# Pool stage by token tiles: own banks for each tile's causal sums, and the band matrix loaded through ScalarE's queue

## The chip, the cores and the metric

The kernel runs on one core of a Trainium2 chip. The time is the device time of one execution in microseconds, median of three runs. The engines are TensorE (PE, with its weight loads as PEld), VectorE (DVE), ScalarE (ACT), GpSimd (POOL) and SyncE (SP), which here only issues transfers. Each runs its own instructions in order and waits on semaphores for the others.

## What is computed

Two stacks of two layers each, on 256 tokens of width 1024, in float32. The first layer's mixer is the part that the change touches: a normalised input, a causal window mean minus the input itself per group of 256 channels (windows 2, 4, 8, 16), one 256x256 product per group, a scale, and the residual.

```python
def pool_mixer(h, w, scale):                 # h = rmsnorm(x, norm_mixer[0])
    csum = concat([zeros, cumsum(h, axis=1)])
    for g, win in enumerate((2, 4, 8, 16)):
        start = maximum(t + 1 - win, 0)
        window_sum = csum[:, 1:, sl] - take(csum[:, :, sl], start)
        outs.append(window_sum / cnt - h[:, :, sl])
    d = stack(outs, axis=2)
    return einsum('btgc,gce->btge', d, w).reshape(B, T, D) * scale

x = x + pool_mixer(...)
x = x + swiglu(rmsnorm(x, norm_ffn[0]), w_gate_up[0], w_down[0])
```

Behind it come a block attention layer and the second stack (three kinds of attention with a latent one, two layers), each with a SwiGLU network. All that is unchanged.

## The kernel before

Tokens lie in two tiles (t = 0, 1) of 128. Every product is made of three float32r matmuls of high and low parts (`three`, lines 1617 to 1619): hi x hi, hi x lo, lo x hi. So an operand has a high half, written by ScalarE (`h_hi`, `whi`), and a low half, the rounding error, written by VectorE (`h_lo`, `wlo`). PSUM has 8 banks of 512 float32 columns; four of them, `ACC` = 4 to 7, hold the stage's output, one for each token tile and half of the width.

The head of the kernel, up to about 23 us, is the pool stage:

- SyncE issues x (two tiles), the gain rows, the band matrix, the pool weights in two halves, the pool scale, then weight units of the first network and many small constants (L516 onwards). GpSimd issues the identity (L612) and two tables.
- The band holds the window weights of each group, 160 columns: 128 for a tile's own tokens, 16 for those of the next tile that still look back into it, and more. VectorE multiplies it by the tokens' 1/rms (`scaled_band`, L1350, L1355), so one matmul with x as weights gives normalised causal sums with channels on partitions (L1817). Tile 0's matmuls are 144 columns wide, to reach the first 16 tokens of tile 1; those of tile 1 are added on top. Banks 0 to 3 hold one group each, both tiles side by side, and a group is ready (`pool_d`) only when tile 1's matmuls are through.
- ScalarE evicts a group with the gain as scale (L832), both tiles at once, and VectorE makes its low half (L1385). ScalarE splits the pool weights' high part in two halves (L824, `pool_whi`), VectorE the low part (L1376, `pool_wlo`).
- PE multiplies (L1617 to L1619), tile and group in the order (0,0), (1,0), (0,1), (1,1), (0,2), (0,3), (1,2), (1,3): 48 matmuls of 256 columns.
- VectorE scales each output (L1139, `pool_scale`) and adds it to x (L1147, `pool_add`); ScalarE squares, VectorE and GpSimd make 1/rms, VectorE normalises (L1046), PE transposes (L1787), and ScalarE and VectorE evict again (L706, L1053) for the first network's weights (L1721).
- To fill time and keep PE at work there are matmuls with zeros (`multiply_zeros`, L1804): 10 and 5 ahead of the causal sums, 6 and 5 behind the pool matmuls, with a small table matmul (L1841) between the last two.

The order on each engine is the order in the text. VectorE's order behind the sums is written in `first_norm`.

Of the kernel before, what the change touches and what calls it, by code (L numbers as in the profile page):

```python
# [24 lines left out]
F32 = mybir.dt.float32  # L25
# [165 lines left out]
def bass_two_stacks(nc, a, c, out):  # L191
    ctx = ExitStack()
    with ctx:
# [3 lines left out]
        def sem(name):  # L197
            return ctx.enter_context(nc.semaphore(name))
# [81 lines left out]
        banks = ctx.enter_context(nc.psum_tensor("bank", [P, 8, HALF], F32))  # L280
        bank = [banks[:, i, :] for i in range(8)]
        ACC = [4, 5, 6, 7]


        vec_dram = nc.dram_tensor("vec_scratch", [24, SEQ_D], F32, kind="Internal")
# [4 lines left out]
        hi_ready, lo_ready, units_used = sem("hi_ready"), sem("lo_ready"), sem("units_used")  # L290
        x_in = [sem("x_in0"), sem("x_in1")]
        small_in, scale_in, ident_in = sem("small_in"), sem("scale_in"), sem("ident_in")
        pool_w_in, pool_hi, pool_lo, pool_out = sem("pool_w_in"), sem("pool_hi"), sem("pool_lo"), sem("pool_out")
        gain_turned, gcol_ready, last_square = sem("gain_turned"), sem("gcol_ready"), sem("last_square")
        table_in, onehot_in = sem("table_in"), sem("onehot_in")
# [159 lines left out]
        def _(sp):  # L455
# [59 lines left out]
            for t in range(TT):  # L515
                sp.dma_start(x[:, t, :], xv[t]).then_inc(x_in[t], 16)  # L516
            sp.dma_start(gain_rows, GAIN_SRC[0].rearrange("(k p) -> k p", p=P)).then_inc(gains_in[0], 16)
            sp.dma_start(band, c["c_band"].rearrange("p g n -> p (g n)")).then_inc(band_in, 16)
            pool_w = raw[:, 0, :].rearrange("p (g k n) -> p (g k) n", g=4, k=2)
            for part, landed in enumerate((pool_w_in, raw_in[0])):  # L520
                sp.dma_start(pool_w[:, 4 * part:4 * part + 4, :],
# [158 lines left out]
        def _(act):  # L680
            def split(n, b=0):

                s = slot_of(n)
                act.wait_ge(raw_in[s], 16 * (n // SLOTS + 1 + b))
                if not (isinstance(b, int) and n + 3 * b < SLOTS):
                    act.wait_ge(units_used, n - 2 + 3 * b)
                w = width_of(n) if isinstance(n, int) else UNIT
                act.activation(whi[:, s, 0:w], raw[:, s, 0:w], ACT.Copy).then_inc(hi_ready, 1)  # L688
# [20 lines left out]
            def norm(j, square_too=True, late_split=None, by_tile=False):  # L709

                by_tile = by_tile or late_split is not None
                for t in range(TT):
                    for h in range(2):
                        if square_too:
                            square(NORM_X[j], t, h)
                    if t == 0 and by_tile:
                        if late_split is not None:
                            split(late_split)
                        for h in range(2):
                            h_out(j, 0, h)  # L720
                for t in range(1 if by_tile else 0, TT):
                    for h in range(2):
                        h_out(j, t, h)
# [88 lines left out]
            act.wait_ge(zeros_set, 1)  # L812
            act.activation(junk[:, 0:T], o_lo[:, 0, :].bitcast(F32), ACT.Square).then_inc(warmed, 1)
            act.wait_ge(warmed, 1)
            for t in range(TT):
                square(0, t, 0, 2)
            act.wait_ge(gain_turned, 1)
# [2 lines left out]
            def pool_whi(part):  # L820

                act.wait_ge((pool_w_in, raw_in[0])[part], 16)
                cols = slice(part * UNIT // 2, (part + 1) * UNIT // 2)
                act.activation(whi[:, 0, cols], raw[:, 0, cols], ACT.Copy).then_inc((pool_hi, hi_ready)[part], 1)  # L824

            act.wait_ge(gcol_ready, 1)
            for k in range(4):
                if k % 2 == 0:
                    pool_whi(k // 2)
                act.wait_ge(pool_d, k + 1)  # L830
                for c_ in (2 * k, 2 * k + 1):
                    i = act.activation(h_hi[:, c_, :], bank[k][:, (c_ % 2) * T:(c_ % 2 + 1) * T], ACT.Copy, scale=gcol[:, c_:c_ + 1])  # L832
                i.then_inc(hT_hi, 1)
            split(1)
            ffn(0)


# [164 lines left out]
        def _(dve):  # L1002
# [108 lines left out]
            def lambdas():  # L1111
# [11 lines left out]
                    dve.tensor_scalar(subln_s[:, l:l + 1], subln[:, l:l + 1], 1.0 - init, None, ALU.mult).then_inc(lam_done, 1)  # L1123
                dve.wait_ge(lam_done, 2)

            def ffn(f):
                u0, e0, g0 = FFN_U[f], NB * f, (NB - 1) * f
                j = [1, 4, 7, 9][f]

                def pool_scale(t, h):  # L1130

                    no = 2 * t + h
                    if no == 0:
                        dve.wait_ge(scale_in, 16)
                    if no < 3:
                        dve.wait_ge(acc_ready, (1, 3, 2)[no])
                    else:
                        dve.wait_ge(units_used, POOL_U + 1)
                    dve.tensor_tensor(pool_y[:, no, :], bank[ACC[no]][:, :],  # L1139
                                      pt[:, h, :], ALU.mult).then_inc(pool_out, 1)  # L1140

                def pool_add(t, h):
# [6 lines left out]
                def first_norm():  # L1149

                    pool_scale(0, 0)
                    pool_add(0, 0)
                    pool_scale(0, 1)
                    pool_add(0, 1)
                    pool_scale(1, 0)
                    mean_square(1, 0)
                    pool_add(1, 0)
                    normalise(1, 0, 0)
                    normalise(1, 0, 1)
                    pool_scale(1, 1)  # L1160
                    pool_add(1, 1)
                    h_lo_out(1, 0, 0)
                    h_lo_out(1, 0, 1)
                    mean_square(1, 1)
                    split_part(u0, 0, 4)
                    normalise(1, 1, 0)
                    normalise(1, 1, 1)
                    for part in range(1, 4):
                        split_part(u0, part, 4)
                    h_lo_out(1, 1, 0)  # L1170
                    h_lo_out(1, 1, 1)
                    split(u0 + 1)
# [190 lines left out]
            second_half_square(0)  # L1363
            dve.wait_ge(last_square, 1)
            mean_square(0, 0)
            second_half_square(1)
            scaled_band(0)
            dve.wait_ge(last_square, 2)
            mean_square(0, 1)
            scaled_band(1)  # L1370

            def pool_wlo(part):
# [3 lines left out]
                dve.tensor_tensor(wlo[:, 0, cols], raw[:, 0, cols], whi[:, 0, cols].bitcast(F32),  # L1376
                                  ALU.subtract).then_inc((pool_lo, lo_ready)[part], 1)

            dve.wait_ge(gcol_ready, 1)
            for k in range(4):  # L1380
                if k % 2 == 0:
                    pool_wlo(k // 2)
                dve.wait_ge(hT_hi, k + 1)
                for c_ in (2 * k, 2 * k + 1):
                    i = dve.scalar_tensor_tensor(out=h_lo[:, c_, :], in0=bank[k][:, (c_ % 2) * T:(c_ % 2 + 1) * T],  # L1385
                                                 scalar=gcol[:, c_:c_ + 1], in1=h_hi[:, c_, :].bitcast(F32),
                                                 op0=ALU.mult, op1=ALU.subtract)
                i.then_inc(hT_lo, 1)
            ffn(0)

            for ev in moba_script():
# [222 lines left out]
        def _(pe):  # L1614
# [187 lines left out]
            def multiply_zeros(n, bk):  # L1802
                for _i in range(n):
                    pe.matmul(bank[bk][:, :], o_lo[:, 0, 0:P], o_lo[:, 0:2, :], start=True, stop=True)  # L1804
# [4 lines left out]
            pe.wait_ge(gains_in[0], 16)  # L1809
            pe.transpose(bank[7][:, 0:KC], gain_rows, ident[0:KC, 0:KC]).then_inc(gain_turned, 1)  # L1810
            multiply_zeros(IDLE_MATMULS[1], 6)
            for s in range(TT):
                width, stride, at = (P, P, P) if s else (P + 16, BAND_W, 0)
                pe.wait_ge(xn_ready, 2 * s + 2)
                for g in range(4):
                    for k in range(2):
                        mm = pe.matmul(bank[g][:, k * T + at:k * T + at + width], x[:, s, g * 256 + k * P:g * 256 + (k + 1) * P],  # L1817
                                       band_s[s][:, g * stride:g * stride + width],
                                       start=(s == 0 and k == 0), stop=(s == 1 and k == 1), skip_group_check=True)
                    if s:  # L1820
                        mm.then_inc(pool_d, 1)
            hi, lo = w8(POOL_U)
            for t, g in ((0, 0), (1, 0), (0, 1), (1, 1), (0, 2), (0, 3), (1, 2), (1, 3)):
                if t == 0:
                    if g % 2 == 0:
                        pe.wait_ge((pool_lo, lo_ready)[g // 2], 1)
                    pe.wait_ge(hT_lo, g + 1)
                for k in range(2):
                    mm = three(bank[ACC[2 * t + g // 2]][:, (g % 2) * 256:(g % 2) * 256 + 256],
                               h_hi[:, 2 * g + k, tile(t)], h_lo[:, 2 * g + k, tile(t)],  # L1830
                               hi[:, 2 * g + k, :], lo[:, 2 * g + k, :], k == 0, k == 1)
                if g % 2 and (t, g) != (1, 3):
                    mm.then_inc(acc_ready, 1)
            used(mm)

            multiply_zeros(IDLE_MATMULS[2], 3)
            pe.wait_ge(ones_set, 2)
            pe.wait_ge(table_in, 32)
            pe.wait_ge(onehot_in, 16)
            pe.wait_ge(pool_out, 3)  # L1840
            pe.matmul(bank[6][0:24, :], tables[:, :], onehots, start=True, stop=True).then_inc(vec_done, 1)  # L1841
            multiply_zeros(IDLE_MATMULS[3], 3)

            def ffn(f):
                u0, e0 = FFN_U[f], NB * f
# [378 lines left out]
```

## Time and profile before

| | us |
|---|---|
| median of 3 runs (1120.51 to 1120.81) | 1120.54 |
| the profiled execution in all | 1121.29 |
| its span, first to last instruction | 1118.9 |
| PE busy | 1107.7 (99%) |
| VectorE busy | 789.5 (71%) |
| ScalarE busy | 539.2 (48%) |

The page divides the span into 40 slices and gives the busy share of each engine in tenths, with the clock that TensorE was granted. The chain of work that ended last is followed back from the last instruction to what released each step. "Busy" of PE is modelled: matmuls overlap, so that 128x256 ones that last 0.28 us each start 0.12 us apart.

### The profile page before, as it was taken

The page shows a single profiled execution, that of the slowest core. Times are in us where ns is not written, and L with a number is a line of the kernel's source. Part 1 is how long each engine was busy: PE and PEld are TensorE (multiplying, and loading weights), DVE is VectorE, ACT ScalarE, POOL GpSimd, SP SyncE. Part 2 cuts the span into 40 slices and gives each one's busy share as a digit, 9 for nine tenths or more (in the row PEclk, how much of TensorE's full clock was granted, in tenths as well). Part 3 has the DMA queues.
Part 4 walks back from the last instruction along what each step waited for, and adds up shares of the span by engine and source line. Part 5 has one row for each costly group of instructions (what it writes and reads, how often), then busy time and mean ns, then how long its engine had stood idle before and what let it go on. Part 6 is the DMA issues. An engine that isn't in the chain of part 4 may idle for free.

```text
span 1118.9 us, 16758 instructions
## 1 busy us (share of the span) xinstructions
PE 1107.7 (99%) x6429; PEld 963.2 (86%) x6429; DVE 789.5 (71%) x1032; ACT 539.2 (48%) x709; POOL 97.1 (9%) x184
## 2 busy tenths in 40 slices
PE   8999999999999999999999999999999999999997
PEld 7888888898888888888998888888899988888886
DVE  6866666767667666678886676666778867766675
ACT  5533333455654333336785543333456755333332
POOL 2000000000000000001660000000036400000000
PEclk9999999999999999999999999999999999999999
DMA  8865565673358556655963465557489444655551
GB/s 258 266 207 191 177 211 189 216 239 113 116 173 278 190 184 200 210 176 145 268 200 118 165 226 188 187 187 217 144 203 264 134 146 161 213 190 187 187 187 37
DMA packets 175974, 211.21 MB, mean 189 GB/s; under 512 B 24467, under 2 KB 159187, under 8 KB 175922
## 3 DMA queue, kind: packets, MB, share of 16 engines
q1 hardware_dynamic: 166146, 202.89, 56.8%
q0 software_dynamic: 9776, 7.62, 3.7%
q8 instruction: 34, 0.56, 0.2%
q14 instruction: 18, 0.15, 0.0%
HBM read 201.98 MB, written 1.16 MB: 182 GB/s over the span
## 4 chain that ended last, share of the span: by engine, by line
PE 96%; DVE 1%; issue 1%; ACT 0%; DMA 0%; POOL 0%; SPq 0%; DVEq 0%; POOLq 0%; ACTq 0%
PE bank L1643 26%; PE bank L1647 14%; PE bank L1617 13%; PE bank L1618 13%; PE bank L1619 13%; PE bank L1721 4%; PE bank L1929 2%; PE bank L1950 2%; PE bank L1656 1%; PE bank L1787 1%; PE bank L1960 1%; PE bank L1682 1%; PE bank L1713 1%; PE bank L1659 1%; PE bank L1964 1%
## 5 line engine op out<-in xcount | busy, mean ns | idle before, releaser
L688 ACT ACTIVATE whi<-raw 128x2048 fp32r<-128x2048 f32 (+2 forms) x180 | 342.0, 1903 | 387.3 <-PE bank L1647 244.9
L1016 DVE TENSOR_TENSOR wlo<-raw,whi 128x2048 fp32r<-128x2048 f32 x175 | 398.2, 2278 | 145.1 <-ACT whi L688 144.7
L1643 PE MATMUL bank<-h_both,whi 128*128 128x512 f32 x1280 | 304.6, 390 | 0.0
L1643 PEld LDWEIGHTS bank<-h_both,whi 128*128 128x128 f32 x1280 | 237.7, 188 | 47.8
L1617 PE MATMUL bank<-whi,o_hi 128*128 128x512 f32 (+1 forms) x452 | 177.4, 392 | 0.0
L1618 PE MATMUL bank<-wlo,o_hi 128*128 128x512 f32 (+1 forms) x452 | 176.0, 389 | 0.0
L1619 PE MATMUL bank<-whi,o_lo 128*128 128x512 f32 x448 | 174.4, 389 | 0.0
L1647 PEld LDWEIGHTS bank<-h_both,wlo 128*128 128x128 f32 x1280 | 164.1, 191 | 6.2
L1647 PE MATMUL bank<-h_both,wlo 128*128 128x256 f32 x1280 | 166.0, 283 | 0.0
L1617 PEld LDWEIGHTS bank<-whi,o_hi 128*128 128x128 f32 x452 | 85.1, 188 | 17.6 <-issue 1.3
L1619 PEld LDWEIGHTS bank<-whi,o_lo 128*128 128x128 f32 x448 | 84.1, 188 | 17.9
L1618 PEld LDWEIGHTS bank<-wlo,o_hi 128*128 128x128 f32 x452 | 85.1, 188 | 15.5
L1221 DVE TENSOR_REDUCE pr<-bank 128x512 f32<-128x1024 f32 x40 | 48.9, 1223 | 47.5 <-PE bank L1647 47.5
L1226 DVE TENSOR_REDUCE pr<-bank 128x512 f32<-128x1024 f32 x36 | 44.1, 1224 | 42.9 <-PE bank L1647 42.9
L622 POOL TENSOR_TENSOR rstd<-msq,neghalf 128x1 f32<-128x1 f32 x16 | 9.6, 599 | 742.1 <-DVE msq L1034 742.1
L1617 PE MATMUL bank<-h_both,whi 128*128 128x256 f32 x192 | 54.8, 286 | 0.0
L796 ACT ACTIVATE pr<-pr,negmax 128x256 f32<-128x256 f32 (+1 forms) x96 | 45.9, 480 | 18.0 <-DVE negmax L1311 18.0
L1618 PE MATMUL bank<-h_both,whi 128*128 128x256 f32 x192 | 54.3, 283 | 0.0
L1619 PE MATMUL bank<-h_both,wlo 128*128 128x256 f32 x192 | 54.3, 283 | 0.0
L1311 DVE CUSTOM_DVE_ANT_0 pr<-bank,bias 128x256 f32<-128x256 f32 (+1 forms) x96 | 32.8, 397 | 12.2 <-PE bank L1929 9.6
L1721 PE MATMUL bank<-whi,h_both 128*128 128x512 f32 x160 | 39.6, 395 | 0.4 <-ACT h_both L706 0.3
L1617 PE MATMUL bank<-whi,h_both 128*128 128x256 f32 (+1 forms) x128 | 39.0, 304 | 0.6 <-DVE h_both L1385 0.6
(202 smaller groups left out, 1330.3 us busy)
## 6 DMA issues: line engine op xcount, KB each, us to landing
raw<-in_w_gate_up SPq DMA_DIRECT2D x44, 1024.0 KB, 5.1
raw<-in_w_down SPq DMA_DIRECT2D x44, 1024.0 KB, 4.9
raw<-in_w_gate SPq DMA_DIRECT2D x22, 1024.0 KB, 5.4
raw<-in_w_up SPq DMA_DIRECT2D x22, 1024.0 KB, 5.3
raw<-in_w_in SPq DMA_DIRECT2D x18, 1024.0 KB, 6.7
raw<-in_w_o SPq DMA_DIRECT2D x12, 1024.0 KB, 4.9
raw<-in_w_kv SPq DMA_DIRECT2D x8, 1024.0 KB, 5.4
raw<-in_w_q SPq DMA_DIRECT2D x4, 1024.0 KB, 5.2
```

Source lines behind the costliest of these rows:

```text
L688: act.activation(whi[:, s, 0:w], raw[:, s, 0:w], ACT.Copy).then_inc(hi_ready, 1)
L796: e = act.activation(pr[:, s, q, 0:w], src, ACT.Exp, bias=negmax[:, s, q:q + 1], scale=-1.0 if biased else 1.0, accum_out=psumrow[:, s, q: ...
L1016: dve.tensor_tensor(wlo[:, s, 0:w], raw[:, s, 0:w], whi[:, s, 0:w].bitcast(F32), ALU.subtract).then_inc(lo_ready, 1)
L1221: dve.tensor_reduce(gate32, halves(0), AX_X, ALU.add).then_inc(gate_sum, 1)
L1226: dve.tensor_reduce(up32, halves(2), AX_X, ALU.add).then_inc(up_sum, 1)
L1311: e = dve.tensor_tensor_reduce(pr[:, s, q, 0:w], bank[i % 2][:, q * T:q * T + w], biases[q], -1.0, BIG, ALU.add, ALU.min, negmax[:, s, q:q ...
L1617: pe.matmul(dst, ahi, bhi, start=first, stop=False)
L1618: pe.matmul(dst, ahi, blo, start=False, stop=False)
L1619: return pe.matmul(dst, alo, bhi, start=False, stop=last)
L1643: pe.matmul(bank[bk + jj][:, :], hi[:, kc, jj * P:(jj + 1) * P], h_both[:, kc, :, :].rearrange("p a t -> p (a t)"), start=(kc == 0), stop= ...
L1647: mm = pe.matmul(bank[bk + jj][:, T:2 * T], lo[:, kc, jj * P:(jj + 1) * P], h_hi[:, kc, :], start=False, stop=(kc == KC - 1))
L1721: mm = pe.matmul(bank[bk][:, :], h[:, kc, tile(t)], pair_of(w, n, kc), start=(first and kc == 0), stop=(last and kc == KC - 1))
```

## The change

Banks: tile 0's own sums go to banks 0 to 3 (256 columns each), tile 1's to banks 6 and 7 (two groups each). The outputs go to `POOL_ACC` = 4, 5, 2, 3. Tile 0's matmuls lose their 16 extra columns, which become eight matmuls of their own into banks 6 and 7. Tile 0 is evicted, given its low half and multiplied as its groups come; tile 1's eviction follows on ScalarE behind both weight halves, and its low half on VectorE behind the scale and add of both halves of tile 0. PE multiplies all of tile 0, then all of tile 1. The split of the first network's first unit moves on ScalarE behind the squares of tile 0. The band's transfer is issued by ScalarE instead of SyncE. VectorE scales the band for tile 0 ahead of the second tile's squares. The idle matmuls behind the stage write bank 0 in place of bank 3, and a wait on `pool_out` ahead of the table matmul goes.

```diff
+        POOL_ACC = [4, 5, 2, 3]
@@ SyncE
-            sp.dma_start(band, c["c_band"]...).then_inc(band_in, 16)
@@ ScalarE: norm(j=1), after the squares of tile 0
                     if t == 0 and by_tile:
+                        if j == 1:
+                            split(FFN_U[0])
                         if late_split is not None:
                             split(late_split)
@@ ScalarE
             act.wait_ge(warmed, 1)
+            act.dma_start(band, c["c_band"]...).then_inc(band_in, 16)
+            def pool_t0_h_hi(g):
+                act.wait_ge(pool_d, g + 1)
+                for k in range(2):
+                    i = act.activation(h_hi[:, 2 * g + k, 0:P], bank[g][:, k * P:(k + 1) * P], ACT.Copy, scale=gcol[...])
+                i.then_inc(pool_t0_hi, 1)
+            def pool_t1_h_hi(half):
+                act.wait_ge(pool_d, 4 + half + 1)
+                for k in range(4):
+                    c_ = 4 * half + k
+                    i = act.activation(h_hi[:, c_, P:2 * P], bank[6 + half][:, k * P:(k + 1) * P], ACT.Copy, scale=gcol[...])
+                i.then_inc(hT_hi, 2)
             act.wait_ge(gcol_ready, 1)
-            for k in range(4):
-                if k % 2 == 0:
-                    pool_whi(k // 2)
-                act.wait_ge(pool_d, k + 1)
-                for c_ in (2 * k, 2 * k + 1):
-                    i = act.activation(h_hi[:, c_, :], bank[k][:, (c_ % 2) * T:(c_ % 2 + 1) * T], ACT.Copy, scale=gcol[...])
-                i.then_inc(hT_hi, 1)
-            split(1)
+            pool_t0_h_hi(0)
+            pool_t0_h_hi(1)
+            pool_whi(0)
+            pool_t0_h_hi(2)
+            pool_t0_h_hi(3)
+            pool_whi(1)
+            pool_t1_h_hi(0)
+            pool_t1_h_hi(1)
@@ VectorE: pool_scale
-                        dve.wait_ge(acc_ready, (1, 3, 2)[no])
+                        dve.wait_ge(acc_ready, (1, 2, 3)[no])
-                    dve.tensor_tensor(pool_y[:, no, :], bank[ACC[no]][:, :],
+                    dve.tensor_tensor(pool_y[:, no, :], bank[POOL_ACC[no]][:, :],
@@ VectorE: first_norm
                     pool_scale(0, 0)
                     pool_add(0, 0)
                     pool_scale(0, 1)
                     pool_add(0, 1)
+                    pool_t1_h_lo(0)
+                    mean_square(1, 0)
+                    pool_t1_h_lo(1)
+                    normalise(1, 0, 0)
                     pool_scale(1, 0)
-                    mean_square(1, 0)
+                    normalise(1, 0, 1)
                     pool_add(1, 0)
-                    normalise(1, 0, 0)
-                    normalise(1, 0, 1)
                     pool_scale(1, 1)
                     pool_add(1, 1)
@@ VectorE: head (pool_t0_h_lo(g): two 128x128 residuals of group g; pool_t1_h_lo(half): four)
             mean_square(0, 0)
+            scaled_band(0)
             second_half_square(1)
-            scaled_band(0)
             dve.wait_ge(last_square, 2)
             mean_square(0, 1)
+            pool_t0_h_lo(0)
             scaled_band(1)
-            (for each k: pool_wlo(k // 2) if k is even; two 128x256 residuals)
+            pool_t0_h_lo(1)
+            pool_wlo(0)
+            pool_t0_h_lo(2)
+            pool_t0_h_lo(3)
+            pool_wlo(1)
@@ PE
-            (tile 0: 8 matmuls of 144 columns; tile 1: 8 of 128; banks 0 to 3)
+            pe.wait_ge(xn_ready, 2)
+            for g in range(4):
+                for k in range(2):
+                    mm = window(g, k * P, 0, 2 * g + k, g * BAND_W, P, k == 0, k == 1)
+                mm.then_inc(pool_d, 1)
+            pe.wait_ge(gcol_ready, 1)
+            for half in range(2):
+                for k in range(4):
+                    window(6 + half, k * P, 0, 4 * half + k, (2 * half + k // 2) * BAND_W + P, 16, k == 0, False)
+            pe.wait_ge(xn_ready, 4)
+            for half in range(2):
+                for k in range(4):
+                    mm = window(6 + half, k * P, 1, 4 * half + k, (2 * half + k // 2) * P, P, False, k == 3)
+                mm.then_inc(pool_d, 1)
-            for t, g in ((0, 0), (1, 0), (0, 1), (1, 1), (0, 2), (0, 3), (1, 2), (1, 3)):
+            for t, g in ((0, 0), (0, 1), (0, 2), (0, 3), (1, 0), (1, 1), (1, 2), (1, 3)):
-                    pe.wait_ge(hT_lo, g + 1)
+                pe.wait_ge((pool_t0_lo, hT_lo)[t], g + 1)
-            multiply_zeros(IDLE_MATMULS[2], 3)
+            multiply_zeros(IDLE_MATMULS[2], 0)
-            pe.wait_ge(pool_out, 3)
             pe.matmul(bank[6][0:24, :], tables[:, :], onehots, start=True, stop=True).then_inc(vec_done, 1)
-            multiply_zeros(IDLE_MATMULS[3], 3)
+            multiply_zeros(IDLE_MATMULS[3], 0)
```

## Rows read from the trace of the kernel before

**Rows 1.** The page: busy time of PE, and the granted clock in 40 slices.
```profile
PE 1107.7 (99%) x6429; PEld 963.2 (86%) x6429; DVE 789.5 (71%) x1032; ACT 539.2 (48%) x709; POOL 97.1 (9%) x184
...
PEclk9999999999999999999999999999999999999999
```

**Rows 2.** Waits of PE, whole kernel: total us, times, longest.
```profile
PE bank L1804 <- DVE o_lo L1339: 1.5, 1, 1.5
...
PE bank L1617 <- DVE h_both L1385: 0.6, 1, 0.6
PE bank L1682 <- DVE h_both L1053: 0.6, 1, 0.6
```

**Rows 3.** Chain that ended last, in order of time: start us, us, what.
```profile
8.92 2.69 PE bank L1817 x20
...
11.62 0.85 ACT h_both L832 x2
...
12.49 0.89 DVE h_both L1385 x2
...
13.52 0.36 PE bank L1617
...
19.51 1.39 PE bank L1804 x6
...
23.22 0.45 PE bank L1787 x4
```

**Rows 4.** Timeline, 0 to 20 us: start us, us, engine, line, operation [idle before].
```profile
0.75 0.86 SPq L516 DMA_DIRECT2D x<-in_x  x2
...
1.47 4.53 PE L1804 MATMUL bank<-o_lo 128*128 128x512 f32 x10 [1.47 <-DVE o_lo L1339]
...
2.04 0.42 ACT L813 ACTIVATE junk<-o_lo 128x256 bf16<-128x256 f32 x1
2.08 0.36 SPq L518 DMA_DIRECT2D qall<-in_c_band  x1
...
4.08 0.69 DVE L1360 CUSTOM_DVE_ANT_0 xn<-x 128x512 f32<-128x512 f32 x1 [2.39 <-DMA x<-in_x]
...
6.63 0.22 PE L1810 MATMUL bank<-ident,xn 8*128 8x8 f32 x1 [0.62 <-DMA ident<-in_c_ident]
6.78 1.43 PE L1804 MATMUL bank<-o_lo 128*128 128x512 f32 x5
...
8.31 0.55 DVE L1350 TENSOR_SCALAR qall<-qall,rstd 128x640 f32<-128x640 f32 x1 [1.79 <-issue]
...
8.92 4.01 PE L1817 MATMUL bank<-qall,x 128*128 128x144 f32 x32 [0.70 <-DVE qall L1350]
...
9.58 1.06 ACT L824 ACTIVATE whi<-raw 128x1024 fp32r<-128x1024 f32 x1 [2.52 <-DMA raw<-in_pool_w]
...
10.74 1.23 DVE L1376 TENSOR_TENSOR wlo<-raw,whi 128x1024 fp32r<-128x1024 f32 x1 [0.47 <-ACT whi L824]
11.62 1.56 ACT L832 ACTIVATE h_both<-bank,gcol 128x256 fp32r<-128x256 f32 x4 [0.99 <-PE bank L1817]
12.49 1.66 DVE L1385 SCALAR_TENSOR_TENSOR h_both<-bank,gcol,h_both 128x256 fp32r<-128x256 f32 x4 [0.53 <-ACT h_both L832]
...
16.88 0.68 DVE L1139 TENSOR_TENSOR pr<-bank,pt 128x512 f32<-128x512 f32 x1
...
18.20 0.68 DVE L1139 TENSOR_TENSOR pr<-bank,pt 128x512 f32<-128x512 f32 x1
```

**Rows 5.** DMA issues, 0 to 40 us: KB each, median us to landing.
```profile
ident<-in_c_ident POOLq DMA_DIRECT2D x1, 64.0 KB, 5.3
```

**Rows 6.** Weight loads by form, whole kernel: busy us, mean ns.
```profile
L1817 PEld LDWEIGHTS bank<-qall,x 128*128 128x128 f32 x32 | 3.8, 191 | 1.1 <-DVE qall L1350 1.1
...
L1962 PEld LDWEIGHTS bank<-pt,vg 128*64 128x64 f32 x32 | 2.8, 137 | 0.8
...
L1841 PEld LDWEIGHTS bank<-bias,tables 97*24 97x24 f32 x2 | 0.1, 101 | 0.4 <-issue 0.4
```

## What the change was expected to do, before it ran

> **What bounds the kernel now.** The page comes first: PE is busy for 99% of the span, and its granted clock stands in the top tenth in all forty slices [rows 1]. So time can be won or lost only where PE waits, or where its queue grows or shrinks. The waits of PE come next [rows 2], each named by the instruction that waited and what it waited for: 1.5 us at the start, 0.6 before the first pool matmul (L1617), and over the rest of the kernel nothing longer than 0.6 us; the timeline adds 0.6 before the identity is there and 0.7 before the first causal sum [rows 4]. Nothing behind the pool stage has slack that could swallow a shift: what the stage loses or wins arrives at the end one for one. The chain of waits is then read for the first 30 us [rows 3]. It runs through the band's transfer (it ends DVE's wait at 8.31), the causal-sum matmuls (8.92), ScalarE's eviction (11.62), VectorE's residual (12.49), 48 pool matmuls from 13.52 to 19.51 (0.36 for the first, so 0.12 for each of 47), and then 11 idle matmuls round the table matmul, up to 23.22, where the transposes of the next norm start. What is on this chain is the whole argument.
>
> **Band and start of the sums.** Let T be the start of the first causal-sum matmul, now 8.92. Three things bound it: the band has landed (8.31, then 0.61 for the scaling and the hand-over), tile 0 is normalised (earlier), and PE is through its own queue. PE waits for the identity until 6.63, then runs five idle matmuls, 6.78 to 8.21 [rows 4]. By their pitch of 0.23 us it could take the next work near 8.05. ScalarE now issues the band after its warm-up at 2.04 + 0.42, about 0.4 us later than SyncE did at 2.08, but it no longer stands behind x in one queue. Bounds for its landing: above, as now, 8.31; below, 2.5 plus the 3.3 us that x's first tile took from issue (0.75) to use (4.08), 5.8 [rows 4]. I take 7.2, the middle. Then the band no longer decides and PE's own queue does: T = 8.05, or a little later if the identity, which shares the transfers' engines with a further queue, is late. I take T = 8.2, with 8.05 and 8.92 as ends. The issue itself, near 0.4 us on ScalarE, is hidden: that engine next waits for x's first tile, which VectorE too has only at 4.08 [rows 4]. SyncE's queue moves up by the same 0.4 us; the pool weights still come after the same bytes, so I leave them at 9.58.
> The Trainium skill (DMA: Bandwidth & Descriptors, Queues, rings and completion order) says that each DMA engine goes round the queues that have work, so a new queue gets a share at once. By that rule 7.2 is right and x's second tile is delayed instead; no row here has such a transfer of this size.
>
> **Causal sums.** Removed: 8 matmuls of 144 columns; added: 8 of 128 and 8 of 16. Each shows as two records, so 32 become 48. Twenty records take 2.69 us and all 32 take 4.01, so the last twelve, 128 wide, cost 0.11 each; the 144-wide cost 0.124 [rows 3, 4]. The trace has no 16-column matmul. Its columns alone would be priced by the difference, 0.014 us a record. But every one needs a weight load of 128 columns, and loads of 24, 64 and 128 columns last 101, 137 and 191 ns [rows 6]: 0.86 ns a column, so 0.11 us of loading each, which is also the pitch of the 128-wide ones. I take 0.11 and keep 0.014 as the lower end (16 records: 1.76 or 0.2 us). From T to the first pool matmul, S: 48 x 0.11 + 0.15 = 5.45, so S = 13.65.
> Beside it: the first group's sums are ready at T + 0.72 (2.69 less 0.44 and 15 x 0.124 leaves 0.39 for the first record, three more). of 128x256 evictions on ScalarE two take 0.85 us and four 1.56, of residuals on VectorE 0.89 and 1.66 [rows 3, 4]: pitches of 0.36 and 0.39, and 0.50 for one alone. No 128x128 one exists; less the 0.11 and 0.13 of 128 columns they would be 0.26, at worst 0.36 and 0.39, at best 0.20. VectorE's order is residual, the band's second half, residual, wlo (1.23), two residuals, wlo: the first wlo is done at T + 4.2, the second at T + 6.5 (its whi, 1.06 us a half [rows 4], is done at T + 5). The first wlo is hidden behind the sums, which are 1.2 us longer. The second is wanted by the 13th pool matmul at S + 1.44 = T + 6.9, so it is hidden too, by 0.3 us; if that goes, PE waits.
>
> **The second tile's wait.** This is the step that decides. Now the pool matmuls alternate between tiles; h_lo of all four groups is made before any VectorE work on the outputs, and PE never stops. After the change PE does all of tile 0 (24 matmuls), then waits for tile 1's residual, which stands on VectorE behind two scale and two add instructions of tile 0. The second scale waits for the 24th matmul itself. So:
> first pool matmul S; 24th done S + 0.36 + 23 x 0.12 = S + 3.1; scale and add, 18.20 - 16.88 = 1.32 from one scale to the next [rows 4], S + 4.45; four 128x128 residuals, 3 x 0.26 + 0.34, S + 5.55; hand-over 0.14, as now from 12.49 + 0.89 to 13.52 [rows 3], S + 5.7; 24 matmuls, 0.35 + 23 x 0.12, S + 8.8.
> Now the last is done at 19.51, which is S' + 6.0 with S' = 13.52. So PE stops for 2.8 us that no filler covers, with S + 2.9 to S + 5.7 idle. The second half's residual (a mean square of 0.2 and four residuals) is done 1.25 us after the first, inside the 1.44 us of PE's twelve matmuls.
>
> **Behind it.** The fillers and the table matmul come after the pool matmuls in PE's order, and their count stands: 23.22 - 19.51 = 3.71 us, unchanged. The dropped wait on pool_out never showed. Tile 0's normalised rows are ready near S + 9, well under the fillers, so what the change frees in that place buys nothing: the fillers were long enough. Scale and add of tile 1 hide there as well (3 us of cover). Behind 23.22 the order is as now, with the next norm's first weights split late enough on ScalarE to be hidden by 4 us.
> Sum: 2.8 + (13.65 - 13.52) = +2.95 us. The profiled execution has a span of 1118.9 and took 1121.29 in all, 0.75 above the median of 1120.54; its analogue after would have a span near 1121.9. On the median: 1120.54 + 2.95 = 1123.5.
>
> **Rivals.**
> A. The forecast, T 8.05 to 8.5 and prices as taken: +2.7 to +3.3, 1123.2 to 1123.8.
> B. Not slower: narrow instructions cost only their columns. Place: the 16 small records on PE, and the 128x128 residuals on VectorE. Price: with 0.014 instead of 0.11, S is set by the first wlo and the 13th matmul by the second, as if S were T + 5.1 (-0.35); residuals at 0.20 take 0.25 off the second tile's wait and 0.5 off the way to the second wlo. With T = 8.05: 2.8 + (13.15 - 13.52) - 0.75 = +1.7, 1122.2. It decides once it gives back 0.75 us. For it: the columns are half and an eighth. Against it: rows 6 for the loads.
> C. The band or the identity is no earlier, or later: T = 8.92 to 9.5. Then +3.7 to +4.25, 1124.2 to 1124.8. For it: transfers issued by GpSimd beside x took 5.3 us for 64 KB [rows 5], so a queue of its own is no guarantee of speed.
> D. The clock. The first ten idle matmuls, after an idle start, took 4.53 us against 1.43 for five later ones [rows 4], 0.45 each against 0.23 to 0.29: at half speed at first, though the page's clock row stays high. If the 2.8 us stop brings that back, 24 matmuls of 256 columns at 0.21 instead of 0.12 cost 2.2 us more, +5.1, 1125.7. The Trainium skill (TensorE: Matmul & The Clock Gate, HAM oscillation) warns of just this, waits between bursts that put the clock back; of the trace of before only the start bears on it, and PE was busy before this stop, where it was cold there.
> E. Something unseen, such as the 0.6 us waits downstream falling away: 0 to -3 us.
>
> **Chances.** A 0.56, B 0.16, C 0.14, D 0.10, E 0.04. A measurement of this kernel tells some 0.2% (2.24 us) from no change. Faster has half of E, 0.02. Within 0.2% is up to 1122.8: B nearly whole and the other half of E, 0.18. Slower: 0.80. The range takes in A, B and C and ends below D: 1122.0 to 1125.1.
>
> **What would show it.** In the new trace: the band scaled before 8.0 and the sums from about 8.2; 48 sum records over 5.4 us; a stop of PE near 16.6 to 19.4, ended by VectorE's residual; the last pool matmul near 22.4 and the transposes near 26.1. I am wrong if the stop is under 1.5 us, if the small matmuls run at a pitch far from 0.11, or if the transposes start within 1 us of 23.2.

## The result

The changed kernel takes 1128.77 us (median of 6 runs, 1127.62 to 1132.32) against 1120.55: ratio 1.008, interval 1.0069 to 1.009, so 8.2 us slower, where 3.0 were forecast, the range ended at 1125.1 and the dearest rival was priced at 5.1. The profiled execution took 1128.51 with a span of 1126.3; before, 1121.29 and 1118.9.

Waits of PE over the whole kernel, after (answers to [rows 2]):

```profile
PE bank L1655 <- DVE h_both L1160: 2.5, 1, 2.5
PE bank L1851 <- DVE qall L1391: 1.8, 1, 1.8
PE bank L1842 <- DVE o_lo L1380: 1.5, 1, 1.5
PE bank L1720 <- DVE h_both L1072: 0.6, 1, 0.6
```

The first line is the forecast stop between the tiles. The second was not forecast: 1.8 us ahead of the causal sums (L1851), waiting for the scaled band. The chain of work that ended last, in order of time (start, us, what; answers to [rows 3]):

```profile
2.49 6.22 DMA qall<-in_c_band
...
9.40 7.08 PE bank L1851 x48
...
20.73 1.13 DVE h_both L1160 x4
21.86 0.04 issue
21.91 0.39 PE bank L1655
22.29 0.12 PE bank L1656
...
22.90 0.21 PE bank L1655
23.11 0.21 PE bank L1656
...
26.30 0.12 PE bank L1656
...
26.54 1.39 PE bank L1842 x6
...
30.25 0.45 PE bank L1825 x4
```

The transposes start at 30.25, before at 23.22: 7.0 us, and nearly the whole of the 7.4 by which the spans differ. The medians differ by 0.8 more than the spans, because the execution of the kernel before that was profiled is 0.75 us above its median. The pool matmuls go at 0.12 us each, then from 22.90 at 0.21, then at 0.12 again; the sums take 7.08 us for 48 records, where the forecast had 5.4. Stretches of the span show why (us; busy time and instructions of PE, weight loads, VectorE, ScalarE, GpSimd; granted clock; DMA share; GB/s):

```profile
7.60:9.40 1.80, 0.00 (x0) 0.00 (x0) 0.60 (x2) 0.00 (x0) 0.00 (x0) 0.91 1.09 391
9.40:12.00 2.60, 2.60 (x12) 2.60 (x13) 1.31 (x6) 1.11 (x4) 1.13 (x2) 0.50 0.94 325
...
19.40:21.90 2.50, 0.00 (x0) 0.00 (x0) 2.47 (x9) 1.77 (x5) 0.00 (x0) 1.00 0.47 84
21.90:22.90 1.00, 0.99 (x7) 0.99 (x8) 1.00 (x5) 1.00 (x1) 0.56 (x1) 0.92 0.17 6
22.90:26.10 3.20, 3.20 (x16) 3.20 (x16) 2.65 (x5) 2.28 (x2) 0.00 (x0) 0.50 0.85 251
```

Twice PE has nothing to do (0.00 busy), and twice the granted clock then stands at 0.50, the lower of the two levels, 1.2 GHz, for some 3 us: from about 9.1, while PE still waits, to 12.4, and from about 22.7, when PE has been at work again for 0.8 us, to 26.1. Before, it was 1.00 in all of this stage. The 7.0 us, piece by piece:

| piece | before | after | difference |
|---|---|---|---|
| start of the sums, T | 8.92 | 9.40 | +0.5 |
| T to the first pool matmul | 4.6 | 6.85 | +2.25 (0.8 for the order of the sums, 1.5 at the low clock) |
| pool matmuls, first to last | 6.0 | 10.3 | +4.3 (2.8 for the stop, 1.5 at the low clock) |
| idle and table matmuls behind | 3.71 | 3.71 | 0 |

The split of the second row comes from seven profiles below in which the clock stayed: there T to the first pool matmul is 5.38 and the 48 records take 5.62 or 5.63. The 16 records more cost PE 1.6 us (5.62 against 4.01 for 32), but half of it comes back, mostly because the first pool matmul no longer waits 0.6 us for its operands [rows 2]. The first row is the difference of two single profiles, and the band was used at 8.31 in that of the kernel before, later than in any of the five other profiles in which SyncE issued it behind x (7.38 to 8.16); by medians the piece is 1.4 (b less d, below).

### The profile page after: what moved, and what is told of

It reads as the page before. It is cut to its first block, busy times and chain, and to the rows that moved or that the text cites. A ratio compares the mean times of both kernels' runs of the same rounds, so it can differ in the third digit from the quotient of the medians.

```text
span 1126.3 us, 16805 instructions
## 1 busy us (share of the span) xinstructions
PE 1112.3 (99%) x6445; PEld 967.6 (86%) x6445; DVE 790.9 (70%) x1040; ACT 540.9 (48%) x717; POOL 96.3 (9%) x184
## 3 DMA queue, kind: packets, MB, share of 16 engines
q0 software_dynamic: 9776, 7.62, 3.7%
## 4 chain that ended last, share of the span: by engine, by line
PE 96%; DVE 1%; issue 1%; ACT 1%; DMA 1%; POOL 0%; DVEq 0%; POOLq 0%; ACTq 0%
PE bank L1681 26%; PE bank L1685 14%; PE bank L1655 13%; PE bank L1656 13%; PE bank L1657 13%; PE bank L1759 4%; PE bank L1973 2%; PE bank L1994 2%; PE bank L1694 1%; PE bank L1825 1%; PE bank L2004 1%; PE bank L1720 1%; PE bank L1751 1%; PE bank L1697 1%; PE bank L2008 1%
```

## The experiments

Theory 1: the stage loses by two stops of PE (the late band, the late low halves of tile 1) and again by the clock that falls after them. Theory 2: the slow records are slow by themselves, through the narrow matmuls or the traffic on the banks. The first four ran on one chip, beside the kernel before at 1120.56 us (20 runs, 1120.34 to 1121.17).

**a_band_sync**, the changed kernel with the band on SyncE again:

```diff
-            act.dma_start(band, ...).then_inc(band_in, 16)
+            sp.dma_start(band, ...).then_inc(band_in, 16)      # behind the gain rows
```

> The changed kernel with one part undone: the band is issued by SyncE again, behind x. Theory 1 (two stops of PE, and the clock that falls after each): the sums start at 8.9 instead of 9.4, the stop before them is under 1.2 us, the clock stays, and the 48 sum records take 5.4 us instead of 7.1. Gain 0.5 + 1.4 = 1.9 us, 1126.6. Theory 2 (the records of the sums are slow by themselves, through the narrow matmuls or the banks): the start gains 0.5, the 7.1 us stay, 1128.1.

Measured: 1125.4 us (1123.77 to 1125.98). More came back than theory 1 said, 3.4 against the changed kernel. The chain of its profiled execution, the 1123.77 one:

```profile
2.08 5.22 DMA qall<-in_c_band
...
7.38 0.56 DVE qall L1391
...
7.99 5.62 PE bank L1851 x48
...
17.85 1.13 DVE h_both L1160 x4
18.98 0.04 issue
19.02 0.39 PE bank L1655
...
22.16 1.39 PE bank L1842 x6
```

The sums start 1.4 us earlier than from ScalarE's queue, and 48 records take 5.62: 0.11 each and 0.3 for the first one's length. So the narrow matmuls cost as much as the 128-wide ones, as the weight-load rows had suggested, and nothing is slow in them beyond that. The stop between the tiles is there in full (2.5 us), but in this execution the clock stayed: 24 matmuls in 3.14. Its other times lie at 1124.2 and 1125.4 to 1126.0. The higher three would fit one fall of the clock, about 1.5 us, but none of them was profiled, so this is not shown.

**b_low_first**, tile 1's low halves ahead of the scale and add of tile 0:

```diff
                 def first_norm():
+                    pool_t1_h_lo(0)
+                    pool_t1_h_lo(1)
                     pool_scale(0, 0)
...
-                    pool_t1_h_lo(0)
                     mean_square(1, 0)
-                    pool_t1_h_lo(1)
```

> The changed kernel with tile 1's low halves made ahead of the scale and add of tile 0 on VectorE. Theory 1: the stop of 2.5 us between the tiles goes, and with it the half clock on 15 pool matmuls (1.5 us): 4.3 us less, 1124.3. Theory 2 (the slow pool matmuls come from the eviction traffic on the banks, not from the stop): only 2.8 us less, 1125.8, and the matmuls of tile 1 are still 0.21 us apart for a stretch.

Measured: 1123.02 us (1122.71 to 1124.35), ratio 1.0023 (1.0013 to 1.0032). The stop is gone from the waits of PE; only the one ahead of the sums is left:

```profile
PE bank L1851 <- DVE qall L1391: 1.7, 1, 1.7
PE bank L1842 <- DVE o_lo L1380: 1.5, 1, 1.5
```

In this profiled execution the clock stayed at 1.00 after that 1.7 us stop; the time was 1.3 us below what was expected, about what one fall costs. The only execution far above the others, 1124.35, has the lowest mean granted clock, 0.997 against 0.998 to 0.999.

**c_fill_stops**, the stops kept and filled with idle matmuls:

```diff
-            multiply_zeros(IDLE_MATMULS[1], 6)
+            multiply_zeros(IDLE_MATMULS[1] + 7, 6)
...
+                if (t, g) == (1, 0):
+                    multiply_zeros(9, 0)
```

> The changed kernel with 7 more idle matmuls ahead of the sums and 9 between the tiles, nothing else. Theory 1: PE is kept at work in both stops, the clock stays at 2.4 GHz, and 1.4 + 1.5 = 2.9 us come back though PE still waits as long: 1125.6. Theory 2: nothing comes back, 1128.5 or more.

Measured: 1125.72 us (1125.47 to 1127.49), 3.1 below the changed kernel's 1128.8. The sums, from the timeline, and two stretches of the profiled execution:

```profile
9.46 5.63 PE L1851 MATMUL bank<-qall,x 128*128 128x128 f32 x48
```

```profile
9.40:12.00 2.60, 2.54 (x23) 2.55 (x23) 1.82 (x7) 1.74 (x5) 1.12 (x2) 1.00 1.00 320
20.50:24.00 3.50, 3.50 (x27) 3.41 (x28) 3.50 (x9) 3.27 (x2) 0.56 (x1) 1.00 0.29 43
```

The sums start at 9.46 and the second tile at 20.50, 5.66 us after the first pool matmul as in the changed kernel, so both as late as without the idle matmuls, and the clock stands at 1.00 in both stretches. Nothing useful was added and nothing waited for came sooner, so what came back is the clock. This decides against theory 2. Against b_low_first it is 2.7 us slower: that is the stop between the tiles by itself, without the clock.

**d_band_and_low**, the edits of a and b together:

> Both edits at once: the band by SyncE, tile 1's low halves first. Theory 1: what stays of the loss is 16 records more in the sums (0.85 us) and what the span shows beside the stage (0.4): 1121.4 to 1121.8, no stop of PE over 1.2 us and the clock at its upper level throughout. Theory 2: 1124 or more.

Measured: 1121.59 us (1120.99 to 1124.56), ratio 1.0012 (1.0003 to 1.0022), as theory 1 has it. Timeline of the profiled execution, the fastest:

```profile
8.00 5.62 PE L1851 MATMUL bank<-qall,x 128*128 128x128 f32 x48 [0.15 <-DVE qall L1391]
...
19.87 3.70 ACT L690 ACTIVATE whi<-raw 128x2048 fp32r<-128x2048 f32 x2
...
22.93 1.03 PE L1825 MATMUL bank<-ident,xn 128*128 128x128 f32 x8
...
23.57 1.09 ACT L708 ACTIVATE h_both<-bank 128x512 fp32r<-128x512 f32 x2
```

In steps of one part each: d is 1.0 above the kernel before (of which the 0.8 between T and the first pool matmul is the part that the profiles show), b is 1.4 above d (the band's queue), c 2.7 above b (the stop), and the changed kernel 3.1 above c (the clock). That is the whole 8.2 us. The 1128.8 comes from other runs than the rest; the changed kernel was therefore run again.

**i_changed_again**, with the kernel before at 1120.77 beside it:

> The changed kernel as it is, on the same chip as the next two. Theory 1: 1127.5 to 1129, with single times apart by about 1.5 us, according to whether the clock fell after none, one or both of the stops.

Measured: 1129.05 us (1127.0 to 1132.45). The profiled execution is the 1127.0 one. Its stretches:

```profile
9.40:12.00 2.60, 2.60 (x25) 2.60 (x25) 1.82 (x8) 1.93 (x5) 1.13 (x2) 1.00 1.02 314
...
19.40:22.00 2.60, 1.71 (x13) 1.71 (x14) 2.60 (x10) 2.60 (x4) 0.56 (x1) 0.97 0.52 79
22.00:24.00 2.00, 2.00 (x12) 2.00 (x11) 2.00 (x4) 1.56 (x1) 0.00 (x0) 0.50 0.55 126
```

Here the clock stayed after the first stop (1.3 us this time) and fell only after the second, at about 21.9, when PE had been at work again for 1.6 us: 25 records in 9.40 to 12.00 where the first profile has 12. That execution was 1.5 us shorter than the first profiled one with two falls. Three executions of this kernel, two of them in the first measurement, are above 1132. None was profiled, but their mean granted clock is 0.993, against 0.995 to 0.997 in the others. By that, an estimate, they spent some 5 to 9 us more at the lower level (0.002 to 0.004 of 1130 us were lost at half speed), which is about the 3.5 us that they are longer than 1128.8; where in the kernel this was is open.

**h_no_idle**, the kernel before with a stop made on purpose:

```diff
-            multiply_zeros(IDLE_MATMULS[1], 6)
+            multiply_zeros(0, 6)
```

> The kernel before without the five idle matmuls ahead of the sums, so that PE stops for about 2 us (6.8 to 8.9) with nothing else changed. Theory 1: in part of the executions the granted clock falls to 1.2 GHz shortly after, some 12 to 15 records of the sums take 0.21 us instead of 0.12, and those executions are up to 1.4 us longer: single times between 1120.5 and 1122, a wider spread than the kernel before. Theory 2 (the clock isn't moved by such a stop): 1120.6 in every execution.

Measured: 1122.14 us (1120.72 to 1123.7), ratio 1.0014 (1.0004 to 1.0024), beside the kernel before at 1120.79 (31 runs, 1120.11 to 1121.31), as it stands beside the next three too. Timeline and stretches of the profiled execution:

```profile
8.23 5.50 PE L1817 MATMUL bank<-qall,x 128*128 128x144 f32 x32 [2.16 <-DVE qall L1350]
```

```profile
7.00:9.00 2.00, 0.77 (x3) 0.77 (x4) 0.71 (x3) 0.00 (x0) 0.62 (x2) 0.72 1.09 384
9.00:11.00 2.00, 2.00 (x10) 2.00 (x9) 1.26 (x3) 1.06 (x1) 0.70 (x1) 0.50 1.01 320
```

The same 32 records take 5.50 us where they took 4.01 [rows 4], after a wait of 2.16. Seven of the ten times are above the 1122 that was named as the upper end. The two highest (1123.44 and 1123.70) have a mean clock of 0.999, so they are long for another reason, which is open. Five idle matmuls, which look like waste, are worth 1.4 us here. The old kernel shows it with no part of the change in it.

**e_band_scalar**, the kernel before with only the band's transfer moved to ScalarE, behind its warm-up:

> The kernel before with the band issued by ScalarE after its warm-up, nothing else. Theory 3 (on a queue of its own the band lands later, because SyncE's long queue of weights takes most turns): the band is scaled at 8.8, 1 us or more later than from SyncE's queue, the sums start at 9.4; 0.5 to 1.4 us slower, 1121.0 to 1122.0, with single executions 1.4 us above that where the clock falls in the longer stop. Rival (the late landing belonged to the changed kernel's other edits, or to the chip it ran on): the sums start as in the kernel before, 1120.6.

Measured: 1122.11 us (1121.54 to 1124.03), ratio 1.0014 (1.0004 to 1.0024). Seven times lie between 1121.5 and 1122.4 with a mean clock of 0.999, three between 1123.5 and 1124.0 with 0.997 or 0.998, and the profiled one is of the three. DMA issue and use of the band in its timeline:

```profile
2.49 0.44 ACTq L814 DMA_DIRECT2D qall<-in_c_band  x1
...
8.90 0.55 DVE L1350 TENSOR_SCALAR qall<-qall,rstd 128x640 f32<-128x640 f32 x1 [2.51 <-issue]
...
9.51 5.61 PE L1817 MATMUL bank<-qall,x 128*128 128x144 f32 x32 [1.88 <-DVE qall L1350]
```

The band is scaled at 8.90, 8.80 in the changed kernel, 8.83, 8.85 and 8.65 in b, c and i; from SyncE's queue at 8.31 in the kernel before and at 7.38, 7.39, 7.62, 7.84 and 8.16 in a, d, h, j and k. So the later landing comes with the move to the other queue, with no other edit, and is 0.3 to 1.5 us, of which 0.4 is the later issue. Again the sums ran at the low clock for a stretch (0.50 from about 9.4 to 12.8), 5.61 us for 32 records.

**f_band_scalar_first**, the same as ScalarE's very first instruction:

> As the last, but the band is ScalarE's first instruction, near 0.8 us, ahead of the warm-up. If only the time of issue matters, it lands 1.7 us earlier than there, near 7.1, and the sums start at 8.0 where PE is free: 1120.0. If the sharing of the engines is what costs, it still lands no earlier than from SyncE's queue (7.4 or later), x lands later, and the time is 1120.5 to 1121.5.

Measured: 1121.19 us (1121.01 to 1122.81), ratio 1.0008 (0.9998 to 1.0017), no clear difference from before. Six times lie at 1121.0 to 1121.2 and four at 1122.6 to 1122.8; the profile is of one of the four. In it the band landed 4.6 us after its issue, near 5.35, earlier than either forecast had it, but VectorE used it only at 7.65, behind its work on x, and now x came late, and the gain rows behind it:

```profile
7.03 0.69 DVE L1360 CUSTOM_DVE_ANT_0 xn<-x 128x512 f32<-128x512 f32 x1 [0.70 <-DMA x<-in_x]
...
7.39 0.24 PE L1810 MATMUL bank<-ident,xn 8*128 8x8 f32 x1 [1.28 <-DMA xn<-in_norm_mixer]
7.56 2.50 PE L1804 MATMUL bank<-o_lo 128*128 128x512 f32 x5
...
9.86 4.44 PE L1817 MATMUL bank<-qall,x 128*128 128x144 f32 x32
```

x's second tile was used from 7.03, where h_no_idle, e_band_scalar and the kernel before have 5.57 to 5.82. PE's small transpose, and the five idle matmuls behind it, moved from 6.63 to 7.39; these took 2.50 us instead of 1.43, though the clock row shows 1.00 there, and the sums began at 9.86. The clock row shows 1.00 beside the ten first idle matmuls too, which ran at the same slow pace, so it does not show every slow stretch; whether the clock fell in the wait of 1.28 us or had not yet risen is open.

**g_band_ahead**, the band on SyncE between the two tiles of x:

> The kernel before with the band in SyncE's queue between the two tiles of x. Within one queue the transfers keep their order, so the band lands before x's second tile, near 6.5, and PE takes up the sums as soon as its idle matmuls end, near 8.0. x's second tile lands 1 us later, which the sums of tile 1 don't feel before 11. Expected 0.3 to 0.9 us faster than the kernel before, 1119.7 to 1120.2. Rival: x's second tile becomes what the sums wait for, no gain.

Measured: 1123.59 us (1121.81 to 1124.95), ratio 1.0023: a miss in sign. The band came in good time (4.0 us after its issue, near 5.2), but the gain rows, 4 KB that stand behind it in the same queue, did not:

```profile
7.86 0.23 PE L1811 MATMUL bank<-ident,xn 8*128 8x8 f32 x1 [2.44 <-DMA xn<-in_norm_mixer]
8.02 2.50 PE L1805 MATMUL bank<-o_lo 128*128 128x512 f32 x5
...
10.32 4.39 PE L1818 MATMUL bank<-qall,x 128*128 128x144 f32 x32
```

PE stopped for 2.44 us, the clock fell (0.50 from about 7.9 on), five idle matmuls took 2.50 us instead of 1.43, and the sums began at 10.32. I had looked at what waits for x and for the band, and not at the third transfer that was moved.

**j_sync_fill**, the band on SyncE and nine idle matmuls between the tiles:

> The changed kernel with the band by SyncE and nine idle matmuls between the tiles: the first stop gone, the second still waited for but filled. Theory 1: what is left is the serial wait for the low halves (2.8 us) and the 16 narrow records (0.85), with no clock in it: 1120.6 + 3.3, 1123.7 to 1124.3, and the single times within 0.6 us of each other, where the band alone gave 1123.8 to 1126.0. Rival (the spread comes from the transfers): the spread stays 2 us.

Measured: 1124.42 us (1123.75 to 1124.98), ratio 1.003 (1.0019 to 1.0041). The spread is 1.2 us, twice what theory 1 named, where a_band_sync, without the idle matmuls, had 2.2: the spread does not come from the clock alone. Each against the kernel before on its own chip, j is 3.65 and d_band_and_low 1.03 above, so the stop between the tiles with no clock in it is 2.6.

**k_less_filler**, d with less filler behind the pool matmuls and the normalisation of tile 0 in one piece:

```diff
-IDLE_MATMULS = (10, 5, 6, 5)
+IDLE_MATMULS = (10, 5, 5, 3)
...
+                    normalise(1, 0, 1)
                     pool_scale(1, 0)
-                    normalise(1, 0, 1)
```

> The band by SyncE, tile 1's low halves first, the second half of tile 0 normalised ahead of the scale of tile 1, and three idle matmuls fewer behind the pool matmuls (5 and 3 in place of 6 and 5). If the fillers were what held the transposes, they start 0.6 us earlier than with both edits alone (22.9): 1121.0. If VectorE holds them there, PE waits for the normalised rows instead and nothing or less than 0.3 us is gained: 1121.3 to 1121.6. The kernel before (1120.6) isn't beaten in either case, unless the transposes start before 22.3.

Measured: 1121.42 us (1121.02 to 1122.35), ratio 1.0005 (0.9996 to 1.0014). Timeline:

```profile
20.65 3.70 ACT L690 ACTIVATE whi<-raw 128x2048 fp32r<-128x2048 f32 x2
...
21.98 1.42 DVE L1065 SCALAR_TENSOR_TENSOR xn<-x,rstd,gains 128x512 f32<-128x512 f32 x2 [0.98 <-DMA gains<-in_norm_ffn]
...
24.97 2.08 PE L1759 MATMUL bank<-whi,h_both 128*128 128x512 f32 x8 [0.87 <-ACT h_both L708]
```

The sums start at 8.76 here and the transposes at 23.01, 14.25 us later; in d it is 14.93 (8.00 to 22.93). So the transposes did come 0.7 us earlier, measured from the sums. But the matmuls behind them come 16.2 to 16.3 us after the sums in both (24.97 here, 24.31 in d): PE waits 0.87 us for ScalarE's eviction, and that starts at 24.26, when the splits of the first network's weights end (two instructions, 3.70 us). In the kernel before one of the two ran at 16.31, ahead of the squares of tile 0, and ScalarE then stood idle for 1.5 us before its eviction; the change put both behind the squares. In d too the eviction starts as the split ends (19.87 + 3.70 = 23.57). VectorE waits for the next gains until 21.98 beside it. What the tile order would bring with that split in its old place was not tried; as it stands, it is no faster than the kernel before.

## Why the prediction was wrong

**Band and start of the sums: the step that failed first.** T was put at 8.2, and was 9.40; of the 4.1 us by which the 7.0 exceed the forecast 2.95, 1.2 are here and 3.0 are the clock. The issue was at 2.49 as said, and x's second tile was no later (used at 5.78, before at 5.82), but the band was used at 8.80, not 7.2. I took the middle between two bounds, and the upper bound, "as now", was not one: a queue of its own made the transfer later. The Trainium skill (DMA: Bandwidth & Descriptors, Queues, rings and completion order) has the engines go round the queues that have work. In f_band_scalar_first the trace agrees: issued beside x, the band landed in 4.6 us and x's second tile was used 1.2 to 1.5 us later than in e, h and the kernel before. Issued at 2.49, behind x, it took 6.1 to 6.3 us (changed kernel, b, c, e, i), where it took 5.2 to 6.1 from SyncE's queue, and x was not held back. The rule gives no order of arrival; how the turns were dealt out is open. The identity was there at 5.96, so PE's own queue ended at 7.57, not 8.05, and the late band left it without work.

**The clock: the term put at nothing.** The sum had no clock in it, and measured it is 3.0 us, 1.5 after each stop. Rival D had it at one chance in ten, for the second stop alone and in place of rival C. The first stop did not exist in my sum, since T was bound by PE's queue there. In the event C's T of 9.40 and D came together, and D twice. The price of the second was put at 2.2 us for 24 matmuls at 0.21; measured it is 1.5, since the first six and the last two still ran at 0.12. The note that PE had been busy before this stop was used as an argument against the fall; the changed kernel itself refutes it, with a fall after the second stop although PE had worked without a gap from 9.40 to 19.4. The Trainium skill (TensorE: Matmul & The Clock Gate, HAM oscillation) warned of waits between bursts of matmuls, and the trace agrees in kind, though its waits are shorter than those of the section's example. Stops of 1.3 and 1.7 us were profiled with the clock staying (and one of 1.3 in f, where the row leaves it open), those of 1.8, 1.9, 2.2, 2.4 and twice 2.5 with a fall, and one of 2.5 (a_band_sync) without, so a stop of 2 us has to be priced with and without it.

**Causal sums: right.** 48 records at 0.11 were said to take 5.4; at full clock they take 5.62 or 5.63 in seven profiles, and T to S is 5.38, where 5.45 was said. The weight-load rows [rows 6] were the right neighbours for a matmul that the trace did not have.

**The second tile's wait: right.** From the first pool matmul to PE's restart S + 5.7 was said, and it is 21.91 - 16.25 = 5.66. Its share of the time is 2.7 (c less b) and 2.6 (j less d, each against the kernel before beside it), where the sum had 2.8.

**Behind it: right for this kernel.** 3.71 us from the last pool matmul to the transposes, unchanged, and the splits on ScalarE were over at 25.2, 5.5 us before its eviction. With the stops gone this cover is used up: in d the splits end as the eviction starts, and in k they are what PE waits for.

The range failed because its cases were taken as alternatives, one chance each, while a stop and the clock after it belong together: in these profiles no stop under 1.8 us has a fall in the clock row, and six of the seven from 1.8 us up have one.

## What to carry to other kernels

Price a stop of the bounding engine twice: its length, and what the clock takes back after it (here about 1.5 us for a stop of 2). Where an order is changed so that one tile finishes first, look at what the second tile's operands stand behind on the engine that makes them: moving them ahead of the first tile's outputs took away the stop of 2.7 us, and with it what the clock took after it. And before a transfer is moved to another queue or another place, list all that lands behind it: here 4 KB of gain rows decided as much as 512 KB of x.

## What the runs showed of the hardware

- After stops of PE of 1.8 to 2.5 us the granted clock went from 1.00 to 0.50 and stayed there for some 3 us (about 9.1 to 12.4 and 22.7 to 26.1 in the changed kernel), in six of seven profiled stops of that length. At the second stop it fell only after PE was back at work, by 0.8 us in one profile of the changed kernel and by 1.6 in the other. At 0.50, sum records of 128 columns start 0.21 us apart instead of 0.11, and pool matmuls of 256 columns 0.21 instead of 0.12.
- A matmul of 16 columns with 128x128 weights costs as much as one of 128 columns of the same kind, 0.11 us a record.
- The 320 KB band is in use 0.3 to 1.5 us later from ScalarE's queue, issued 0.4 us later, than from SyncE's behind x (five profiles against six). Issued at 0.75 on ScalarE's queue, beside x, it lands in 4.6 us, and x's second tile is in use 1.2 to 1.5 us later.
- With the band ahead of the 4 KB of gain rows in SyncE's queue, PE could transpose them only at 7.86; with the band behind them it did so at 5.85 to 6.63.
